# A two-block transformer in fp32 on one core: the input moved to the head of the weight queue, and the first modulation group summed by TensorE in four 32-column groups

## The reference, cut to what matters

```python
silu_c = jax.nn.silu(c)
for i in range(DEPTH):
    mod = silu_c @ ada_w[i] + ada_b[i]
    sh_t, sc_t, ga_t, sh_c, sc_c, ga_c = jnp.split(mod, N_MOD, axis=-1)
    hn = modulate(rms_norm(x, norm_tm_g[i]), sh_t, sc_t)
    ...
# the first mixer
xx = 0.5 * (x_prev + x_next) - h
xs = h[:, :, None, :] + xx[:, :, None, :] * mu
rkv = jnp.einsum('bsjd,jde->bsje', xs[:, :, :3], w_rkv)
```

## Time and profile before

| | us |
|---|---|
| median of 3 runs | 2935.41 |
| lowest, highest | 2929.65, 2935.97 |
| span of the profiled execution | 2930.1 |

### The profile page before, as it was taken

One profiled execution on the slowest core, in us unless ns is written; L12 is line 12 of the kernel. 1 busy time (PEld: TensorE's weight loads), 2 busy tenths in 40 slices (PEclk: granted clock), 3 DMA queues, 4 the chain that ended last, 5 costly groups with the idle time before them and its releaser, 6 DMA issues.

```text
span 2930.1 us, 52775 instructions
## 1 busy us (share of the span) xinstructions
PE 2793.3 (95%) x21826; PEld 2485.1 (85%) x21826; DVE 2161.7 (74%) x2714; ACT 1632.9 (56%) x2317; POOL 159.4 (5%) x164
## 2 busy tenths in 40 slices
PE   6889999999999999999999999999999999999999
PEld 5877777778778999878787888999999979998998
DVE  7868875899996656689998666666666786668665
ACT  2445543788884444478888544445544824446443
POOL 0024430000000020100000000000000000000000
PEclk8989999999999999999999999999999999999999
DMA  7601124699995736179998413554455404544453
GB/s 318 237 2 46 60 74 155 232 354 350 356 354 192 273 132 243 44 288 353 356 357 339 187 58 118 185 186 147 155 186 187 157 12 177 186 159 142 148 185 129
DMA packets 78260, 572.73 MB, mean 195 GB/s; under 512 B 8802, under 2 KB 8930, under 8 KB 9186
## 3 DMA queue, kind: packets, MB, share of 16 engines
q1 hardware_dynamic: 76752, 558.93, 51.3%
q10 hardware_dynamic: 1298, 10.83, 0.9%
HBM read 568.67 MB, written 1.05 MB: 194 GB/s over the span
## 4 chain that ended last, share of the span: by engine, by line
PE 82%; DVE 12%; ACT 3%; DMA 1%; issue 1%; POOL 0%; DVEq 0%; SPq 0%; ACTq 0%; PEldq 0%
PE ps L1377 14%; PE ps L1299 13%; PE ps L1254 8%; PE ps L1398 7%; PE ps L863 5%; PE ps L865 5%; PE ps L864 5%; PE ps L1255 4%; DVE arena L2245 4%; DVE wl L2239 2%; DVE arena L2239 2%; PE ps L1497 1%; DMA ring<-in_stream 1%; PE ps L898 1%; PE ps L897 1%; PE ps L896 1%
## 5 line engine op out<-in xcount | busy, mean ns | idle before, releaser
L2239 DVE TENSOR_TENSOR wl<-ring,wh 128x1024 fp32r<-128x1024 f32 (+1 forms) x560 | 938.2, 1695 | 366.1 <-ACT wh L1636 345.6
L1636 ACT ACTIVATE wh<-ring 128x1024 fp32r<-128x1024 f32 (+1 forms) x560 | 789.5, 1432 | 454.4 <-PE ps L1255 209.6
L1254 PE MATMUL ps<-hx,wh 128*128 128x512 f32 x1024 | 362.4, 396 | 1.3 <-DVE wl L2239 1.3
L863 PE MATMUL ps<-hx,wh 128*128 128x256 f32 x1072 | 310.6, 290 | 22.5 <-DVE hx L2239 17.4
L864 PE MATMUL ps<-hx,wl 128*128 128x256 f32 x1072 | 306.5, 286 | 0.0
L865 PE MATMUL ps<-hx,wh 128*128 128x256 f32 x1072 | 306.3, 286 | 0.0
L1299 PE MATMUL ps<-hidh,wh 128*128 128x256 f32 x1024 | 290.4, 284 | 1.1 <-DVE hidl L2239 1.1
L1299 PE MATMUL ps<-hidl,wh 128*128 128x256 f32 x1024 | 289.8, 283 | 0.0
L1299 PE MATMUL ps<-hidh,wl 128*128 128x256 f32 x1024 | 289.7, 283 | 0.0
L1255 PE MATMUL ps<-hx,wl 128*128 128x256 f32 x1024 | 287.1, 280 | 0.0
L1633 ACT ACTIVATE arena<-arena 128x256 f32<-128x256 f32 (+7 forms) x420 | 207.2, 498 | 97.5 <-DVEq L2766 33.8
(11 more groups left out here) (286 smaller groups left out, 5662.0 us busy)
## 6 DMA issues: line engine op xcount, KB each, us to landing
ring<-in_stream SPq DMA_DIRECT2D x532, 1024.0 KB, 4.9
arena<-in_wcmp ACTq DMA_DIRECT2D x2, 2048.0 KB, 10.5
arena<-in_lora ACTq DMA_DIRECT2D x1, 2048.0 KB, 9.8
arena<-in_atm ACTq DMA_DIRECT2D x1, 1762.0 KB, 11.6
x<-in_xT ACTq DMA_DIRECT2D x1, 1024.0 KB
out<-x SPq DMA_DIRECT2D x1, 1024.0 KB, 3.9
arena<-in_rwm ACTq DMA_DIRECT2D x1, 736.0 KB, 12.8
cols<-in_cols ACTq DMA_DIRECT2D x1, 715.0 KB
```

What stands on the lines that cost most here:

```text
L863: mm(out, w[0], h[0], start=first, stop=False)
L1254: mm(o.rearrange("p (a s) -> p a s", a=2), w[0], hx[:, :, k, :], start=k == 0, stop=False, skip_group_check=True)
L1636: return nc.scalar.activation(out, in_, ACT.Copy)
L2239: return v.tensor_tensor(out, a, b, op)
```

## The change

The input x becomes the first transfer of SyncE's queue, ahead of the stream, with a semaphore of its own, for which ScalarE waits before the squares; `cs` then counts three transfers. VectorE no longer sums the first eight blocks. TensorE does it in `ada_first`: for each block, four matmuls of 512 columns straight from the ring, each with a stationary operand of 32 equal columns (128 values of silu(c)), into partitions 32j to 32j+31 of PSUM bank 7, accumulated over the eight blocks. Three fillers follow each block but the last. ScalarE waits for the eighth block, copies the bank to `ADAR` and only then prepares weight blocks 0 and 1. TensorE turns `ADAR` by four transposes into the tile that the modulation is read from, then does ten fillers. Three events are merged with others or dropped.

```diff
@@ -547,7 +547,8 @@
-        ADA_AT = {0: mixa.take(BLK), 1: arena[:, 2064:4112], 4: arena[:, 2064:4112], 5: arena[:, 2064:4112]}
+        ADAR = mixa.take(512)
+        ADA_AT = {1: arena[:, 2064:4112], 4: arena[:, 2064:4112], 5: arena[:, 2064:4112]}
@@ -586,7 +587,7 @@
-        c_landed = sem("c_landed")
+        c_landed, x_landed = sem("c_landed"), sem("x_landed")
@@ -629,7 +630,7 @@
                 what, q = LOADS[n]
-                if what == "ada" and ADA_LIST[q][0] in ADA_AT:
+                if what == "ada" and (ADA_LIST[q][0] == 0 or ADA_LIST[q][0] in ADA_AT):
                     sp.wait_ge(ada_used, q + 1)
                     return
@@ -649,6 +650,7 @@
+            sp.dma_start(x[:, :, :], d["xT"].rearrange("p (c s) -> p c s", c=C)).then_inc(x_landed, 16)
             more = None
             for n, (what, q) in enumerate(LOADS):
@@ -769,7 +771,7 @@
-        CS_N = 64
+        CS_N = 48
@@ -961,16 +963,30 @@
+            def ada_first():
+                pe.wait_ge(ev("start"), 1)
+                for k in range(C):
+                    n = POS["ada", k]
+                    pe.wait_ge(landed[n % RING], 16 * (n // RING + 1))
+                    for j in range(4):
+                        last = mm(ps[32 * j:32 * j + 32, 7, :], silc[:, k:k + 1].to_broadcast([P, 32]), ring[:, n % RING, 512 * j:512 * j + 512],
+                                  start=k == 0, stop=k == C - 1, skip_group_check=True)
+                    last.then_inc(ada_used, 1)
+                    if k < C - 1:
+                        kept_busy(3, ps[:, 6, :])
+                pe.wait_ge(ev("ada_rows"), 1)
+                t = claim("lo", LO["ada0"])
+                for i in range(4):
+                    last = nc.tensor.transpose(t[:, i * P:(i + 1) * P], ADAR[:, i * P:(i + 1) * P], ident)
+                last.then_inc(tile_ready["lo"], 1)
+                kept_busy(10, ps[:, 6, :])
+
             def ada(name, first=0, end=None):
...
                     g = ADA_SUMS[name][o // n16]
-                    if g == 0 and o == 0:
-                        for a in range(2, C - 1):
-                            pe.wait_ge(ada_used, a + 1)
-                            kept_busy(3)
                     if o == first or o % n16 == 0:
@@ -1603,7 +1619,7 @@
             pe.wait_ge(cs, CS_N)
-            steps = {"ada0": lambda: ada("ada0"),
+            steps = {"ada0": ada_first,
...
@@ -1723,7 +1739,7 @@
                 act.sem_inc(ev("lora_ready"), 1)
-                act.wait_ge(ev("lora_w"), 1)
+                act.wait_ge(ev("lora_ready"), 2)
                 ready(act, "lo", m + 2)
@@ -1732,7 +1748,7 @@
                 act.wait_ge(rw_side, 32)
-                act.wait_ge(ev("start"), 1)
+                act.wait_ge(ev("start"), 2)
@@ -2182,7 +2198,6 @@
             act.dma_start(cols[:, 0:C], d["cols"][:, 0:C]).then_inc(c_landed, 16)
-            act.dma_start(x[:, :, :], d["xT"].rearrange("p (c s) -> p c s", c=C)).then_inc(cs, 16)
             act.dma_start(mats[:, :], d["mats"]).then_inc(cs, 16)
@@ -2190,8 +2205,10 @@
             act.wait_ge(c_landed, 16)
             fn(silc, col("c", 0, C), ACT.Exp, scale=-1.0).then_inc(ev("c_exp"), 1)
-            act.wait_ge(cs, CS_N)
+            act.wait_ge(x_landed, 16)
             def ada0():
+                act.wait_ge(ada_used, C)
+                copy(ADAR, ps[:, 7, :]).then_inc(ev("ada_rows"), 1)
                 prep(0)
                 prep(1)
@@ -2333,7 +2350,7 @@
-            ada_done = [0]
+            ada_done = [C]
@@ -2357,7 +2374,11 @@
                     a = slice(16 * (g % 3), 16 * (g % 3) + 16)
-                    K(tt(mod[:, g // 3, a], tile("lo", m)[:, 16 * n:16 * n + 16], col(f"ada_b{g // 3}", a.start, 16), ADD))
+                    t = tile("lo", m)[:, 16 * n:16 * n + 16]
+                    if g == 0:
+                        t = tile("lo", m).rearrange("p (i j r) -> p j i r", i=4, j=4)[:, :, :, 0]
+                    by = [b.rearrange("p (j i) -> p j i", j=4) if g == 0 else b for b in (mod[:, g // 3, a], col(f"ada_b{g // 3}", a.start, 16))]
+                    K(tt(by[0], t, by[1], ADD))
@@ -2365,7 +2386,6 @@
             def ada0():
-                ada_blocks(C)
                 dve.wait_ge(ev("rstd"), 1)
@@ -2428,7 +2448,6 @@
-                dve.sem_inc(ev("lora_w"), 1)
                 dve.sem_inc(ev("lora_ready"), 1)
@@ -3090,6 +3109,7 @@
             K(tt(silc, silc, col("c", 0, C), MUL))
+            dve.sem_inc(ev("start"), 1)
@@ -3173,7 +3193,6 @@
-            pool.sem_inc(ev("hid_wide"), 1)
             pool.sem_inc(ev("hidden"), 1)
```

More of the change, by code:

```diff
@@ L1605, in _ @@
             pe.wait_ge(cs, CS_N)
-            steps = {"ada0": lambda: ada("ada0"), "ada4": lambda: ada("ada4"), "ada5": lambda: ada("ada5"), "mix": mix, "rwkv": rwkv, "nsa": lambda: (woven("nsa"), nsa_compress_values()),
+            steps = {"ada0": ada_first, "ada4": lambda: ada("ada4"), "ada5": lambda: ada("ada5"), "mix": mix, "rwkv": rwkv, "nsa": lambda: (woven("nsa"), nsa_compress_values()),
                      "moba": block_attention, "sb": stick, "convn": lambda: (conv_taps(), conv_norm()),
```

## The result

The changed kernel takes 2936.70 us at the median (20 runs, 2930.09 to 2947.99) against 2931.87 for the kernel before (20 runs, 2921.47 to 2938.62): ratio 1.0021, 95% interval 1.0011 to 1.0031, so 3 to 9 us slower. The forecast was 2938.7, 3.3 us slower, in a range of 2930 to 2948.

A forecast was written before the change was run, and what follows sets the result against it. The prediction took TensorE, 82% of the chain, as the bound, so the start of the first dense matmul moves everything behind it. The modulation coming 3.3 us later gave 2935.4 + 3.3 = 2938.7 us, range 2930 to 2948.

The forecast's parts named there:

- Constants at 13.3: Opening: without x on ScalarE's queue the constants land earlier, so TensorE starts its norm at 13.3 us instead of 19.04.
- Norm 6.0 us: TensorE's norm after idle time takes 6.0 us, ending at 19.3; bounds 3.5 at full rate, 6.9 at the low one.
- Four groups at the price of one, 0.87 us, changes of shape 0.3: TensorE's sums: four groups run together, 0.87 us a block (bounds 0.86 and 3.46); two array shape changes add 0.3.
- the pairwise rival: TensorE's sums: four groups run only two at a time, 0.87 us more a block, +6.9, 2945.6 us; chance 0.08.
- the serial one: TensorE's sums: groups run one after another, 2.59 us more a block, +20.7, 2959.4 us; chance 0.07.
- The rival of a low clock: TensorE's clock is low through the sums, as narrow groups may let it fall: 16 us more, 2954.6; chance 0.05.
- Loads hidden by the fillers: SyncE's loads pause for the ring, but blocks land before TensorE wants them: the fifth near 25.5, wanted at 29 us.
- Eviction, split, low half in a row behind the eighth sum: After sums end at 37.8: eviction 0.60, split 1.91, VectorE's low half 2.28, modulation starting at 42.65 us.
- First tile again at the low clock: First dense tile: after 4.4 idle us the clock is low again, nothing gained; bounds -2.8 to +0.9 us.
- Sum +3.3 us: Whole kernel: the modulation starts 3.3 us later than at 39.25, carried one to one into the time, 2938.7 us.
- the upper bound: Modulation at most +6.5 us, time 2942: norm 6.9 us, shape changes twice as dear, start 0.5 us off.
- The rival of late constants: Opening: moving x brings the constants no earlier, norm at 18.3, 5 us later, time 2943.7 us; chance 0.03.

The follow-up runs named there:

- the repeat: The changed kernel unaltered, timed and profiled a second time against the kernel before: ratio 1.0009 (0.9989 to 1.0030).
- the serial kernel: Changed kernel with each block's four matmuls in one 32-column group and four small evictions in place of one; ratio to the kernel before 1.0076 (two runs).
- reordered: Changed kernel with the norm waiting for the matrices alone, two fillers between blocks, 20 behind the transposes, modulation ahead of VectorE's low half; ratio to before 0.9988.
- the norm early: Changed kernel with block 0's split ahead of the eviction and TensorE's norm waiting for the matrices alone; ratio to the kernel before 0.9996.
- the split first: Changed kernel with ScalarE's split of weight block 0 ahead of its wait for the eighth sum and the eviction; ratio to the kernel before 0.9988.

## Why the prediction was right, point by point

- *Constants at 13.3:* 13.36. The queues took turns packet by packet, as assumed, whatever a packet holds: SyncE's and ScalarE's moved 283 and 287 packets from 5 to 12 us, with 2.07 and 0.87 MB. Up to 12 us SyncE's had moved 3.15 MB, the figure of the sum (with 0.88 of ScalarE's 0.93). The window from 5 to 12 us, then from 0 to 12:

```profile
q1 hardware_dynamic: 283, 2.07, 70.1%
q10 hardware_dynamic: 287, 0.87, 30.8%
...
q1 hardware_dynamic: 418, 3.15, 65.4%
q10 hardware_dynamic: 406, 0.88, 18.5%
```

- *Norm 6.0 us:* 5.1 to 6.5 where the norm came after idle time; 5.1 in the first profile. This is the term that was mis-sized for it. Its records run at four a us at first and then at twice that rate, from about 17 us in the first profile, and only from 19 in the repeat (the granted clock is shown as 1.00 throughout, so this is read from the records' rate alone). It makes the forecast of the modulation 0.9 us too late (42.6 against 41.68). In the repeat the forecast was 0.4 too early.
- *Four groups at the price of one, 0.87 us, changes of shape 0.3:* together 1.17 forecast, 0.99 and 1.49 measured for block and fillers, so 2.49 for the pair against 2.47. The lower bound was right. The serial and the pairwise rival were wrong; that the serial one was well priced (20.7 us) shows in the sums of the serial kernel, which took 20.5 more. The Trainium skill's figure for packed groups ("TensorE: Matmul & The Clock Gate", Part 3), by which I had an estimated 1.13 us a block ahead of the changes of shape, was further off than the row of the halves. The rule of the Trainium skill, "TensorEngine Tiling (Array Packing)", Key Properties, that a change of tiling mode drains TensorE, agrees with the trace, which puts about 0.15 us on a change: 2.49 us a block and its fillers, less 1.30 for the fillers and 0.87 for a block without a change (four in a row took 3.64, with a last record's tail), leaves 0.32 for two changes.
- *The clock holds through the sums:* it did, at 1.00 up to 45 us, with records at the full rate from 17 us. The rival of a low clock was wrong.
- *Loads hidden by the fillers:* yes, and without the fillers they set the pace.
- *Eviction, split, low half in a row behind the eighth sum:* 0.50, 1.90 and 2.2 us on the chain, as forecast. VectorE's freed time gave nothing: it waited from 26.7 to 39.47.
- *First tile again at the low clock:* yes, granted 0.50 until 57.4 us; a gain of 0 was right.
- *Sum +3.3 us:* the profile has +2.5, the repeat +2.5 at the later tile. The timed difference is 3 to 9 us by the first comparison, -3 to +9 by the repeat, and at one clock 1.9 and 3.0 us (estimates). So the mechanism and its size are shown, and nothing speaks for a further loss behind the opening: past 150 us the profiles differ by their time at the low clock. That 2936.70 lies only 2.0 us under the forecast of 2938.7 is in part luck: the kernel before came down from 2935.41 (three runs) to 2931.87 (twenty), and the difference of the medians came out at 4.8 in place of 3.3.
- *The bounds and the chances as written:* the upper bound is added up too low. Norm +0.9, changes +2.2 and start +0.5 give +6.9 at the modulation, not +6.5, and the first tile's +0.9 isn't in the 2942. The rival of late constants (2943.7, so 8.3 us over) is counted under "same" though it lies beyond 0.2%. Neither bears on the result.
- *Chances:* 0.67 for within 0.2% and 0.27 for slower; the ratio of 1.0021 lies on the border between them (the forecast of 3.3 us is 0.11%).

## What to carry to other kernels

Moving work from a busy engine to an idle one moves its place in the order too: here the sums left VectorE, where they had overlapped the loads, and came behind the norm on TensorE and in front of a split on ScalarE, so the chain grew although the work shrank. Look for the first wait of the chain and ask what of it is really read: a separate semaphore for 192 KB brought the modulation forward by 4.4 us, more than the change as a whole was late (2.4), and the later tile by 2.2. Try the parts of a change alone and together: here the early input alone gave nothing, the sum alone lost 7 to 8 us, and they began to pay only when the norm's wait and the order behind the sums were changed too ("reordered": 5.7 us at the later tile). And when run times spread, compare them at the same granted clock: differences of 3 us that the medians hide come out of the same runs.

## What the runs showed of the hardware that was not expected

- Four 32-column groups with all 128 rows and 512 fp32 columns each took 0.91 us (back to back) to 0.99 us (between fillers) for what took 3.55 in a row, so 3.6 times as fast between fillers, with four separate moving streams:

```profile
L972 PE MATMUL ps<-ring,small x64: 592/604/617, 18.5 to 36.4; 128*32 128x512 f32 x64
```

- The clock in a stretch where TensorE is busy 39 to 49% of the time in bursts of six matmuls can fall or hold in kernels with the same order of instructions: with the norm early it fell to 0.50 at 45 us, with the split first it held at 1.00, and both had fillers up to 2 us before the first part.
- The length of the norm's eight matmuls after idle time varied from 5.1 to 6.5 us from one profiled execution to the next, by when the rate of their records doubled.
- Two queues with work took turns packet by packet whatever the packets held: 283 packets with 2.07 MB beside 287 with 0.87 MB in 7 us.
- The spread of this kernel's time, 2920 to 2951 us, follows the time that TensorE spends at the low clock: 0.4 us for each us of it (2.35 us for 0.001 of the mean clock, over 109 runs).
